# A two-layer decoder trunk on one core: sums of down-projection weight blocks made by adding DMAs from GpSimd's queue instead of by VectorE

## The reference, cut to what matters

```python
def squared_relu_mlp(h, w_up, w_down):
    a = jax.nn.relu(h @ w_up)
    return (a * a) @ w_down

def reference(x, ...):
    for layer in range(DEPTH):                      # DEPTH = 2
        g = norm_gains[layer]
        mix = ...                                   # attention on rmsnorm(x, g[0])
        x = x + rmsnorm(mix, g[1])
        hn = rmsnorm(x, g[2])
        x = x + rmsnorm(squared_relu_mlp(hn, w_mlp_up[layer], w_mlp_down[layer]), g[3])
    return x
```

## Time and profile before

| | |
|---|---|
| median of 3 runs | 1075.85 us (1075.31 to 1076.31) |
| the profiled execution | 1075.44 us, of which 1073.6 us are the span from its first to its last instruction |
| busy share of the span | PE 98%, PEld 80%, DVE 70%, ACT 50%, POOL 18% |
| DMA | 99.94 MB, 93 GB/s on average |
| granted TensorE clock | 0.997 of full speed |

### The profile page before, as it was taken

The page is one execution under the profiler, slowest core; times in us unless marked ns, Lnnn a source line. Parts: engine busy times, 40 slices in busy tenths (PEclk is TensorE's granted clock), DMA queues, the critical chain, the costliest instruction groups (busy, mean ns, idle before and its releaser), DMA issues.

```text
span 1073.6 us, 14865 instructions
## 1 busy us (share of the span) xinstructions
PE 1056.8 (98%) x5408; PEld 859.5 (80%) x5408; DVE 748.7 (70%) x1286; ACT 538.6 (50%) x1016; POOL 189.3 (18%) x333
## 2 busy tenths in 40 slices
PE   9999999999999999999999999999999999999997
PEld 8877779888888888888778766679888888888886
DVE  5455636596697696687589898526596696696685
ACT  6677645253453453425554567745254443453422
POOL 0464320000000000005413387520000000000005
PEclk9999999999999999999999999999999999999999
DMA  9531505544535445422613333006553535535402
GB/s 301 115 79 41 118 1 133 123 100 97 115 82 118 105 92 118 96 62 53 140 36 79 79 79 80 1 1 144 112 111 86 118 79 118 115 82 118 106 12 79
DMA packets 52009, 99.94 MB, mean 93 GB/s; under 512 B 4704, under 2 KB 4832, under 8 KB 51936
## 3 DMA queue, kind: packets, MB, share of 16 engines
q1 hardware_dynamic: 51216, 98.61, 40.4%
q10 hardware_dynamic: 720, 0.38, 0.1%
HBM read 96.88 MB, written 2.10 MB: 92 GB/s over the span
## 4 chain that ended last, share of the span: by engine, by line
PE 91%; DVE 5%; issue 1%; ACT 1%; DMA 1%; POOL 0%; DVEq 0%; POOLq 0%; SPq 0%; ACTq 0%
PE bank L2062 11%; PE bank L2060 11%; PE bank L2061 11%; PE bank L2437 7%; PE bank L2435 7%; PE bank L2436 7%; PE bank L2070 6%; PE bank L2072 6%; PE bank L2071 6%; PE bank L2219 3%; PE bank L2461 2%; PE bank L2460 2%; PE bank L2459 2%; PE bank L2288 2%; PE bank L2274 2%
## 5 line engine op out<-in xcount | busy, mean ns | idle before, releaser
L2060 PE MATMUL bank<-r_hi,w_hi 128*128 128x512 f32 (+1 forms) x456 | 177.5, 389 | 0.0
L2061 PE MATMUL bank<-r_hi,w_lo 128*128 128x512 f32 (+1 forms) x456 | 177.4, 389 | 0.0
L2062 PE MATMUL bank<-r_lo,w_hi 128*128 128x512 f32 (+1 forms) x456 | 177.4, 389 | 0.0
L1651 DVE TENSOR_TENSOR w_lo<-w_raw,w_hi 128x1024 fp32r<-128x1024 f32 x84 | 102.0, 1222 | 70.9 <-ACT w_hi L1170 70.7
L1170 ACT ACTIVATE w_hi<-w_raw 128x1024 fp32r<-128x1024 f32 x84 | 88.0, 1056 | 119.4 <-PE bank L2062 82.9
L2435 PE MATMUL bank<-w_hi,hid_hi 128*128 128x512 f32 x336 | 130.7, 389 | 0.0
L2436 PE MATMUL bank<-w_lo,hid_hi 128*128 128x512 f32 x336 | 130.7, 389 | 0.0
L2437 PE MATMUL bank<-w_hi,hid_lo 128*128 128x512 f32 x336 | 130.7, 389 | 0.0
L1179 ACT ACTIVATE w_hi<-w_raw,gT 128x512 fp32r<-128x512 f32 x96 | 64.5, 716 | 106.6 <-DMA w_raw<-in_w_mlp_up 75.1
L814 POOL TENSOR_TENSOR acc<-acc,G 128x512 f32<-128x512 f32 x8 | 13.0, 1651 | 594.3 <-ACT waste L1026 594.3
L2062 PEld LDWEIGHTS bank<-r_lo,w_hi 128*128 128x128 f32 (+1 forms) x456 | 85.2, 187 | 18.2
(11 more groups left out here) (215 smaller groups left out, 2149.4 us busy)
## 6 DMA issues: line engine op xcount, KB each, us to landing
w_raw<-in_w_mlp_up SPq DMA_DIRECT2D x64, 512.0 KB, 6.4
w_raw<-in_w_mlp_down SPq DMA_DIRECT2D x64, 512.0 KB, 6.9
w_raw<-in_b_w_in SPq DMA_DIRECT2D x16, 512.0 KB, 6.8
w_raw<-in_a_w_in SPq DMA_DIRECT2D x8, 512.0 KB, 9.3
w_raw<-in_a_w_out SPq DMA_DIRECT2D x8, 512.0 KB, 5.8
w_raw<-in_b_w_out SPq DMA_DIRECT2D x8, 512.0 KB, 6.0
xt<-in_x_turned SPq DMA_DIRECT2D x8, 256.0 KB, 4.9
X<-in_x SPq DMA_DIRECT2D x4, 512.0 KB, 11.1
```

The source lines that it names most:

```text
L1651: nc.vector.tensor_tensor(half_of(w_lo[:, u % 2, :], a), b_of(PRODUCTS[i][1], a), half_of(w_hi[:, u % 2, :], a).bitcast(f32), ALU.subtract ...
L2060: nc.tensor.matmul(bank, whi, xhi, start=start, stop=False)
L2061: nc.tensor.matmul(bank, wlo, xhi, start=False, stop=False)
L2062: return nc.tensor.matmul(bank, whi, xlo, start=False, stop=stop)
```

## The change

The four weight sums of a quarter are no longer made by VectorE. GpSimd issues DMAs that add their source to what lies at the destination (`accum_op=ALU.add`). An adding DMA can only add, so the sign of B12 is turned in the algebra: T1 = B11 + B12, T2 = T1 + B22, T3 = B22 + B12, T4 = B21 + T2, and the signs of S1, S4 and three of the totals change to match. The number of matmuls and of VectorE additions in `totals` is the same.

T1, T2 and T3 add a block read once more from HBM; T4 adds T2 from SBUF. B12 has no buffer any more: SP now loads B22 a second time, into T3's place, and later than it loaded B12. All four sums wait for, and are waited for as, whole blocks and no longer as halves.

```diff
@@ raw_loads: the order of the loads
-                order += [((layer, n, "B22"), 2), ((layer, n, "B11"), 1), (up_unit(layer, n + 1, 0), 4), ((layer, n, "B12"), 0)]
+                order += [((layer, n, "B22"), 2), ((layer, n, "B11"), 1), (up_unit(layer, n + 1, 0), 4), ((layer, n, "T3"), 3)]
@@ load_mlp, on SP
-                    sp.wait_ge(*t_of(layer, q, "T1", 1))
-                    sp.wait_ge(*t_of(layer, q, "T3", 1))
+                    if q:
+                        sp.wait_ge(b_lo_done, part_no(layer, q - 1, 6, 1))
                     fetch_down(q, "B21")
...
                     sp.wait_ge(b_lo_done, part_no(layer, q, 3, 1))
-                    sp.wait_ge(*t_of(layer, q, "T3", 1))
                     if n < LAST:
                         fetch_down(n, "B22")
-                        sp.wait_ge(*t_of(layer, q, "T4", 1))
+                        sp.wait_ge(*t_of(layer, q, "T4"))
                         fetch_down(n, "B11")
                         sp.wait_ge(*low_of(up_unit(layer, n, 3)))
                         fetch_up(n + 1, 0)
-                        sp.wait_ge(b_lo_done, part_no(layer, q, 6, 1))
-                        fetch_down(n, "B12")
+                        sp.wait_ge(b_lo_done, part_no(layer, q, 5, 1))
+                        fetch_t3(n)
@@ on GpSimd, after x_squares of each layer
+            def added(name, src, done):
+
+                dst = raw(B_PLACE[name]).rearrange("p (k n) -> p k n", k=4)
+                for a in range(2):
+                    rows = slice(64 * a, 64 * a + 64)
+                    nc.gpsimd.dma_start(dst[rows], src[rows], accum_op=ALU.add).then_inc(done, 16)
+
+            def weight_sums(layer, q):
+
+                pool.wait_ge(*loaded((layer, q, "T3")))
+                added("T3", down_block(layer, q, "B12"), t3_made)
+                pool.wait_ge(b_lo_done, part_no(layer, q, 0, 1))
+                added("T1", down_block(layer, q, "B12"), t_made)
+                pool.wait_ge(b_lo_done, part_no(layer, q, 1, 1))
+                added("T2", down_block(layer, q, "B22"), t_made)
+                pool.wait_ge(b_lo_done, part_no(layer, q, 4, 1))
+                added("T4", raw(B_PLACE["T2"]).rearrange("p (k n) -> p k n", k=4), t4_made)
@@ b_high, on ACT
-                    act.wait_ge(*t_of(layer, q, name, a))
+                    act.wait_ge(*t_of(layer, q, name))
@@ on VectorE: weight_sum and t3_sum and their calls are gone; for T2 for instance
-                    for a in range(2):
-                        b_low(layer, q, 1, a)
-                        weight_sum(layer, q, "T2", a)
+                    b_lows(q, 1)
```

More of the change, by code:

```diff
@@ L87, in mlp_role @@
     return what, q + (what == "up"), n
-B_PLACE = {"B12": 0, "T1": 1, "B21": 0, "T4": 0, "B11": 1, "T2": 1, "B22": 2, "T3": 3}
+B_PLACE = {"T1": 1, "B21": 0, "T4": 0, "B11": 1, "T2": 1, "B22": 2, "T3": 3}
 DOWN_PLACE = (2, 1, 3, 0)
@@ L99, in raw_loads @@
         order += [(up_unit(layer, 0, n), n % 2) for n in range(UPS)]
-        order += [((layer, 0, "B22"), 2), (up_unit(layer, 1, 0), 4), ((layer, 0, "B12"), 0), ((layer, 0, "B11"), 1)]
+        order += [((layer, 0, "B22"), 2), ((layer, 0, "T3"), 3), ((layer, 0, "B11"), 1), (up_unit(layer, 1, 0), 4)]
         for q in range(LAST):
@@ L662, in fetch_up, with fetch_t3 @@
                     fetch(up_unit(layer, q, n), up_source(q, n))
+                def fetch_t3(q):
+                    fetch((layer, q, "T3"), down_source(q, 1, 1))
                 def fetch_down(q, b):
@@ L670, in load_mlp @@
                 fetch_down(0, "B22")
-                sp.wait_ge(*low_of(up_unit(layer, 0, 2)))
-                fetch_down(0, "B12")
+                sp.wait_ge(pv_done, PT_AT[16 * (layer + 1)])
+                fetch_t3(0)
                 sp.wait_ge(*low_of(up_unit(layer, 0, 3)))
@@ L927, in _ @@
                 x_squares(layer)
+                for q in range(LAST):
+                    weight_sums(layer, q)
             for j in range(NB):
@@ L1667, in hidden_sum @@
                         dve.wait_ge(a_lo_done, part_no(layer, q - 1, 3, a))
-                    args = a_of("S4", a), a_of("A12", a), a_of("S2", a), ALU.subtract
+                    args = a_of("S4", a), a_of("A12", a), a_of("S2", a), ALU.add
                 nc.vector.tensor_tensor(*args).then_inc(s_made, 1)
[L1671 to L1687, removed]
             def s3_sum(layer, q):
@@ L1694, in s3_sum @@
                     nc.vector.tensor_tensor(a_of("S3", a), a_of("A11", a), a_of("A21", a), ALU.subtract).then_inc(s3_made, 1)
[L1696 to L1702, removed]
-                for a in range(2):
-                    nc.vector.tensor_tensor(b_of("T3", a), b_of("B22", a), b_of("B12", a), ALU.subtract).then_inc(t3_made, 1)
             def taken(layer, q, i):
@@ L1767, in mlp @@
                 s3_sum(layer, 0)
-                t3_sum(layer, 0)
                 b_lows(0, 0)
-                for a in range(2):
-                    weight_sum(layer, 0, "T1", a)
                 for t in range(4, 8):
@@ L1776, in mlp @@
                     up_split(layer, n, 0, (0, 1))
[L1777 to L1780, removed]
                     for a in range(2):
@@ L1813, in mlp @@
                     a_lows(q, 6)
-                    for a in range(2):
-                        b_low(layer, q, 4, a)
-                        weight_sum(layer, q, "T4", a)
+                    b_lows(q, 4)
                     up_split(layer, n, 3, range(4))
```

25 lines of the change are left out of this document (15 added, 10 removed).

## The result

The changed kernel takes 1157.62 us (median of 4 runs, 1156.11 to 1159.20) against 1075.84 us of the kernel before on the same chip: a ratio of 1.0757, 95% interval 1.0743 to 1.0770. I had predicted 1075.9, in a range of 1073 to 1125.

The account below looks back on a forecast made before the run. PE, full in the quarters, was taken as the bound: 56 us of hidden VectorE time, 24 hidden adding pairs and 18 more megabytes from HBM each count 0, so 1075.9 us against a median of 1075.85, range 1073 to 1125.

Parts of the forecast that it names:

- PE bounds the quarters: In layer 0's three quarters PE has no gap; a quarter's 360 matmuls at 0.227 us take 81.6 us.
- VectorE's 56 us are worth nothing: Removing 48 VectorE additions of 1.18 us in six quarters gains 0, since all lie under a full PE.
- 2 + A: Cost of one adding DMA pair: 2 us from issue to data, then its data time; 8 us for a pair.
- A: Data time of an adding DMA pair, taken as 6 us; bounds 4.9 below, 9.8 or 14.7 above.
- rival 1: T1 late behind T3 at the turn to quarters 1 and 2, both layers: 1088 to 1112 us; chance 0.24.
- The chain at the turn to quarter 2: T4, three SP loads, T3, then T1: T1 lands at 390.4, needed by 393.4, so PE never waits.
- the spare of 3.0: At the turn to quarter 2, T1 lands at 390.4 us and is needed by 393.4 for part 1.
- covered up to A = 13: At the turn to quarter 2, B11 lands at 363.9 behind T4, before ScalarE first reads it at 371.46.
- T1 in time: In quarter 0 T1 has the queue for itself and lands at 217.0, against 232.48 less 2.3.
- T2 in time: In quarter 0 T2, beside SP's pairs, lands near 240.5, before its need for part 2 at 246.5.
- the spare of 6 us: In quarter 0, the time between T2's landing near 240.5 and its need at 246.5 for part 2.
- Rival 2: Second reading costs as much as the first: part 1 starts 15.5 us late, four times, 1138 us; chance 0.12.

Follow-up runs that it names:

- both edits: The changed kernel with 1472 instead of 1024 bytes of descriptor room for GpSimd's queue and T1, T2 issued before T3: 1076.67 us, ratio 1.0004.

## Why the prediction was wrong, point by point

**PE bounds the quarters; VectorE's 56 us are worth nothing: right.** VectorE fell by 56.7 us. With both edits it stands at 693.6 us and the time is that of the kernel before.

**An adding pair is 2 + A, A = 6: nearly right in A for HBM, wrong in its form. This is the step that failed.** A measured 6.8 as two single halves, and 6.4 for a pair issued back to back with the larger queue (T1 of quarter 0, windows from 210 to 218 us with both edits: shares 0.15, 1.00, 1.14, 0.90). By the sum that rival 1 used, T1 lands at 354.4 + 6 x 6.4 = 392.8, still in time; at 6.8 it is 2 us late, not 18. What failed is how the pair was put together: I costed a pair as 2 us and then A, that is with both halves in flight. In the change each half has its own 2 us, and the second is issued only when the first has landed, 2 x 5.9 = 11.8 us for an undisturbed pair instead of 8. The trace of before could not show it, since GpSimd issued no DMA of this kind in the quarters; I bounded A from both sides and gave the queue no term at all.

**The chain at the turn to quarter 2: right in its links, too short in each.**

| link | predicted | measured | too short by |
|---|---|---|---|
| T4, issue to landing | 8.0 | 11.9 (370.67 to 382.60) | 3.9 |
| three loads by SP | 16.4 | 18.0 (to 400.62) | 1.6 |
| T3, issue to T1's issue | 8.0 | 19.7 (to 420.31) | 11.7 |
| T1, issue to landing | 8.7 | 12.1 (to 432.36) | 3.4 |

Together 20.6 us, less the spare of 3.0, gives 17.6: the wait of 17.8. The largest is T3's: its first half takes 5.95 us, as an undisturbed one does, and the serial second half, issued at 406.57, takes 13.7, since it meets SP's loads of 404 to 407, which I had let meet only T1's end. T4's 3.9 are the source in SBUF. I had written that T4 was covered up to A = 13, but that was said of B11's load, not of the chain through the raw T3, where A counted from T4 on.

**Quarter 0: T1 in time, right; T2 in time, wrong for the small queue.** T1's data end near 221, against my 217.0 and a need at 230.2. I had T2 landed near 240.5. With room for two halves it is split from 240.85. In the change, with one half at a time, it is split from 246.73, and part 2 starts at 249.47: the spare of 6 us is used up to the last half microsecond. I had looked no further than part 2. What ScalarE does behind T2 is late for up 2, and that costs 2.3 us in the two layers.

**Rival 1 (0.24) named the right mechanism and place:** T1 late behind T3 at part 1 of quarters 1 and 2, four times, nothing in quarter 0. Its price was tied to A alone, so the largest time that I let it reach, 1125 at A = 8.4 (its own sum gives 354.4 + 6 x 8.4 - 393.4 = 11.4 us a wait and 1121.5), was passed although A was 6.4 to 6.8. The experiment that moves T1 ahead of T3 confirms it: no wait is left. Rival 2 would have put the same waits down to a second reading at full price; for T1 and T3 A says no, and only T4, from SBUF, has the 9.9 that it took for all. My sign for telling the two apart was wrong as well: I had written that the length of the wait says A. By that sum 17.8 us would say A = 9.5 (354.4 + 6A = 393.4 + 17.8), where 6.4 to 6.8 were measured.

**The clock was left out.** Neither my case nor the rivals priced what follows a wait: the granted clock goes to 0.50 in it, and the first ten matmuls or so follow each other at 0.43 us. That is 9.0 us of the 80.7.

**The range was too narrow.** It ended at 1125, where the best rival ended. A margin of 3 us in a chain of 44 whose four links all rested on an operation that the trace did not show needed a term for a queue that is not as deep as SP's.

## What to carry to other kernels

When work goes to a queue that the trace has not shown, ask how many of its transfers can be in flight before asking how fast one is, and look in the trace for "issue" in front of the second. What is wanted first has to stand first in an in-order queue: moving T3's two lines behind T2's here gave back 77 of 82 us. And work that is hidden under a full engine isn't worth moving: at best the new place is hidden as well.

## What the runs showed of the hardware

- The halves of an adding pair (512 KB, rows of 2 KB) were issued one at a time with a descriptor room of 1024 and two at a time with 1472. Plain halves of the same shape went up to three at a time with 1024, though not always. Adding halves with rows of 8 KB (T4) went two at a time with 1024, and of T4's eight pieces with rows of 2 KB the first seven.
- An adding pair from HBM takes 6.4 to 6.8 us of data time against 4.9 plain; SBUF to SBUF it takes 9.9 against 4.9.
- GpSimd is busy 1.03 us to issue one adding half, 0.63 us for a plain one.
- After a wait of 17 us PE starts at a granted clock of 0.50, with matmuls 0.43 us apart, and the 24 matmuls of the part take 7.2 to 8.1 us instead of 5.44. The price doesn't shrink with the wait: four waits of up to 17.8 us cost 9.0 us so, four of up to 10.5 us 8.6 (larger room), four of up to 7.5 us 8.8 (T4 on VectorE).
